# Prompt's spectral products on GpSimd, and an output projection that starts on half of its input

## The reference

```
def bidir_long_conv(u, filt):
    ...
    uf = jnp.fft.rfft(u.astype(jnp.float32), n=2 * L, axis=1)
    kf = jnp.fft.rfft(k2, n=2 * L, axis=0)
    return jnp.fft.irfft(uf * kf[None], n=2 * L, axis=1)[:, :L]

def hyena(...):
    u = h @ in_w + in_b
    up = jnp.pad(u, ((0, 0), (1, 1), (0, 0)))
    u = up[:, :-2] * conv_w[0] + up[:, 1:-1] * conv_w[1] + up[:, 2:] * conv_w[2] + conv_b
    x0, x1, v = jnp.split(u, 3, axis=-1)
    zz = v * x1
    y = bidir_long_conv(zz, filt).astype(h.dtype) + zz * dskip
    return (x0 * y) @ out_w
```

## Time and profile before

| | us |
|---|---|
| median of 3 runs (890.23 to 892.2) | 890.26 |
| the profiled execution | 887.65 |
| its span in the trace | 885.8 |
| TensorE busy | 833.5 (94%) |
| VectorE busy | 230.7 (26%) |
| ScalarE busy | 164.6 (19%) |
| GpSimd busy | 38.1 (4%) |

### The profile page before, as it was taken

One profiled execution on the slowest core, in us unless ns is written; L12 is line 12 of the kernel. 1 busy time (PEld: TensorE's weight loads), 2 busy tenths in 40 slices (PEclk: granted clock), 3 DMA queues, 4 the chain that ended last, 5 costly groups with the idle time before them and its releaser, 6 DMA issues.

```text
span 885.8 us, 13072 instructions
## 1 busy us (share of the span) xinstructions
PE 833.5 (94%) x5672; PEld 526.5 (59%) x5672; DVE 230.7 (26%) x462; ACT 164.6 (19%) x313; POOL 38.1 (4%) x67
## 2 busy tenths in 40 slices
PE   4899999899899999999996999999899999999997
PEld 3776777787654455535544888778654554355534
DVE  1245523504611011100103344491420111011003
ACT  3146113521510000000002211400311000000001
POOL 5000000030300000000000000000120000000000
PEclk9999999999999999999998999999999999999999
DMA  9979866734989999999999945537469999999991
GB/s 314 387 255 360 306 247 216 285 140 139 428 329 426 418 427 428 428 430 429 428 407 387 362 154 184 196 107 274 161 255 425 424 431 424 431 428 428 428 425 56
DMA packets 59969, 292.48 MB, mean 330 GB/s; under 512 B 2961, under 2 KB 5126, under 8 KB 47572
## 3 DMA queue, kind: packets, MB, share of 16 engines
q1 hardware_dynamic: 57908, 289.69, 81.8%
q0 software_dynamic: 768, 1.04, 0.5%
q10 hardware_dynamic: 1248, 1.08, 0.4%
HBM read 290.10 MB, written 1.70 MB: 329 GB/s over the span
## 4 chain that ended last, share of the span: by engine, by line
PE 73%; DMA 15%; DVE 6%; ACT 4%; issue 1%; SPq 0%; POOL 0%; DVEq 0%; POOLq 0%
PE ps L1821 21%; DMA ring<-in_moe_w_up 12%; PE ps L1844 9%; PE ps L1940 8%; PE ps L1405 5%; PE ps L1808 4%; PE ps L1862 4%; PE ps L1595 3%; PE ps L1683 3%; PE ps L1467 3%; PE ps L1450 2%; PE ps L1473 2%; DMA ring<-in_ab_in_w 2%; ACT arena L559 1%; DVE xT L1127 1%
## 5 line engine op out<-in xcount | busy, mean ns | idle before, releaser
L1821 PE MATMUL ps<-ring,arena 128*64 128x512 f32 x1024 | 224.2, 593 | 5.5 <-DMA ring<-in_moe_w_up 3.7
L1821 PEld LDWEIGHTS ps<-ring,arena 128*64 128x64 f32 x1024 | 77.4, 137 | 148.0 <-issue 146.0
L1844 PE MATMUL ps<-ring,arena 128*64 128x512 f32 x512 | 113.4, 595 | 1.1 <-ACT arena L782 1.1
L1940 PE MATMUL ps<-hT,ring 128*128 128x256 f32 x384 | 84.1, 380 | 0.3 <-ACT modT L621 0.3
L1940 PEld LDWEIGHTS ps<-hT,ring 128*128 128x128 f32 x384 | 72.6, 190 | 11.4 <-issue 1.2
L1844 PEld LDWEIGHTS ps<-ring,arena 128*64 128x64 f32 x512 | 36.2, 137 | 66.4 <-issue 63.1
L1239 DVE TENSOR_TENSOR arena<-ps,arena 128x256 f32<-128x256 f32 x32 | 18.1, 607 | 218.4 <-PE ps L1821 218.4
L1808 PE MATMUL ps<-arena 128*128 (+1 forms) x512 | 59.9, 275 | 2.1 <-ACT arena L767 2.1
L1808 PEld LDWEIGHTS ps<-arena 128*128 128x128 f32 x512 | 58.4, 192 | 2.2 <-DVE arena L1217 2.2
L1862 PE MATMUL ps<-arena 128*128 (+1 forms) x256 | 59.5, 386 | 0.0
L1405 PE MATMUL ps<-ring,csil 128*32 128x128 f32 x1536 | 51.9, 290 | 7.8 <-ACT modT L621 3.9
(11 more groups left out here) (294 smaller groups left out, 695.8 us busy)
## 6 DMA issues: line engine op xcount, KB each, us to landing
ring<-in_moe_w_gate SPq DMA_DIRECT2D x32, 2048.0 KB, 14.4
ring<-in_moe_w_up SPq DMA_DIRECT2D x32, 2048.0 KB, 17.3
ring<-in_moe_w_down SPq DMA_DIRECT2D x32, 2048.0 KB, 12.8
ring<-in_mod_w SPq DMA_DIRECT2D x24, 2048.0 KB, 11.9
ring<-in_ab_in_w SPq DMA_DIRECT2D x6, 2048.0 KB, 18.1
ring<-in_hy_in_w SPq DMA_DIRECT2D x6, 2048.0 KB, 17.3
ring<-in_ab_out_w SPq DMA_DIRECT2D x2, 2048.0 KB, 11.5
ring<-in_hy_out_w SPq DMA_DIRECT2D x2, 2048.0 KB, 8.4
```

The lines of the kernel that those rows point to most:

```text
L1821: ins = mm(bank(4 + w)[e * 64:e * 64 + 64, :], xg[:, k, e * 64:e * 64 + 64], unit(n + 2 * w + e)[:, k, :], start=(k == 0), stop=(k == KD - 1))
L1844: ins = mm(bank(6 + half)[e * 64:e * 64 + 64, :], hidT[:, f, e * 64:e * 64 + 64], down_unit(n + 4 + e)[:, f, half * 512:half * 512 + 512], ...
L1940: ins = mm(bank(4 + j % 4)[:, 0:256], unit(n)[:, k, (j % 4) * 128:(j % 4) * 128 + 128], hk(k), start=(k == KORDER[0]), stop=(k == KORDER[-1]))
```

## The change

VectorE no longer makes the prompt's product. GpSimd makes it, in six tensor_tensor instructions behind its work for the experts of layer 0; all their inputs and outputs lie in SBUF. VectorE makes only the sample's two halves, behind convolutions 21 and 22. TensorE's inverse transform of the prompt waits for GpSimd's semaphore. For the sample, VectorE's last two instructions are cut in two, four chunks of channels each, and the output projection's first group of matmuls waits for the first four before k = 0 and for the others before k = 4.

```
 # GpSimd, behind the gates of the experts, layer 0
+                if l == 0:
+                    pool.wait_ge(q["a_spec"], 2)
+                    (Ua, Ub), (ya, yb) = U0, YS[0]
+                    g.tensor_tensor(ya, Ua, H["KA"], ALU.mult)
+                    link(pool, "g_chain", g.tensor_tensor(yb, Ub, H["KB"], ALU.mult))
+                    g.tensor_tensor(ya, ya, yb, ALU.subtract)
+                    link(pool, "g_chain", g.tensor_tensor(Ub, Ub, H["KC"], ALU.mult))
+                    link(pool, "g_chain", g.tensor_tensor(yb, Ua, H["KB"], ALU.mult))
+                    g.tensor_tensor(yb, yb, Ub, ALU.add).then_inc(q["g_fb"], 1)
...
 # VectorE
-            def spectral(s, part):
-                if s:
-                    dve.wait_ge(q["t_spec"], 2)
-                    Ua, Ub = bank(0, 2), bank(2, 2)
-                else:
-                    dve.wait_ge(q["a_spec"], 2)
-                    Ua, Ub = U0
-                ya, yb = YS[s]
+            def spectral(part):
+                dve.wait_ge(q["t_spec"], 2)
+                Ua, Ub = bank(0, 2), bank(2, 2)
+                ya, yb = YS[1]
...
-                if 19 <= j <= 22:
-                    spectral((j - 19) // 2, (j - 19) % 2)
+                if j in (21, 22):
+                    spectral(j - 21)
...
-                L(v.tensor_tensor(z4, z4, bank(4 + 2 * s, 2).rearrange("p (k t) -> p k t", k=KD), ALU.add))
-                v.tensor_tensor(x04, x04, z4, ALU.mult).then_inc(q["d_r"], 1)
+                y4 = bank(4 + 2 * s, 2).rearrange("p (k t) -> p k t", k=KD)
+                for ks in [slice(0, 4), slice(4, 8)] if s else [slice(0, 8)]:
+                    L(v.tensor_tensor(z4[:, ks], z4[:, ks], y4[:, ks], ALU.add))
+                    v.tensor_tensor(x04[:, ks], x04[:, ks], z4[:, ks], ALU.mult).then_inc(q["d_r"], 1)
...
 # TensorE
             for s in range(NS):
-                pe.wait_ge(q["d_spec"], s + 1)
+                if s == 0:
+                    pe.wait_ge(q["g_fb"], 2)
+                else:
+                    pe.wait_ge(q["d_spec"], 1)
...
-            pe.wait_ge(q["d_r"], 2)
-            out_projection(OUT1_AT, [0, 1, 2, 3], lambda k: H["x0"][:, k * 256:k * 256 + 256], mod_step)
+            def mixed_ready(k8, k):
+                if k8 == 0 and k % 4 == 0:
+                    pe.wait_ge(q["d_r"], 2 + k // 4)
+            out_projection(OUT1_AT, [0, 1, 2, 3], lambda k: H["x0"][:, k * 256:k * 256 + 256], mod_step, mixed_ready)
```

More of the change, by code:

```diff
@@ L1308, in spectral @@
                     v.tensor_tensor(yb, yb, t1, ALU.add).then_inc(q["d_spec"], 1)
-                    dve.wait_ge(q["d_spec"], s + 1)
+                    dve.wait_ge(q["d_spec"], 1)
             for j in range(24):
@@ L1673, in _, with out_projection @@
             pe.wait_ge(q["a_cat"], 2)
-            def out_projection(at_unit, banks, src, between=lambda c: None):
+            def out_projection(at_unit, banks, src, between=lambda c: None, ready=lambda k8, k: None):
                 for half in range(2):
@@ L1682, in out_projection @@
                         for k in range(KD):
+                            ready(k8, k)
                             ins = mm(out, unit(n)[:, k, c * 128:c * 128 + 128], src(k), start=(k == 0), stop=(k == KD - 1))
```

## The result

The changed kernel takes 896.67 us (median of 14 runs) where the kernel before takes 891.88 on the same chips: ratio 1.0049, 95% interval 1.0036 to 1.0062, so 4.4 us slower (3.2 to 5.5). On the 890.26 of the forecast that is 894.6, the number predicted. A second comparison gave 1.0041 (1.0027 to 1.0055).

What follows compares the result with a forecast made beforehand. TensorE was taken as the bound, with 1.90 us of waits to win; turns between GpSimd and VectorE, less the split, gave +2.85 us, with the clock's fall +4.36, so 890.26 + 4.36 = 894.6 us, range 890.2 to 896.3.

Steps and rivals of the forecast that it cites:

- Only 1.9 us to win: TensorE stood still 1.21 us before the sample's inverse transform and 0.69 before the output projection; 1.90 us is all to win.
- VectorE and GpSimd take turns, for whole instructions: In convolutions 20 and 21 VectorE's six instructions alternate with GpSimd's six; VectorE 7.3 us late, TensorE idle 4.5 us.
- tensor_scalar takes turns too: First instruction of convolutions 20 and 21, one input at two elements a cycle, also waits for GpSimd; its turn 0.27 us.
- rival 2: tensor_scalar of convolutions 20 and 21 does not wait for GpSimd, two turns fewer: +0.4, 890.7 us; chance 0.15.
- GpSimd's instruction, 2.09 us: Each GpSimd tensor_tensor of 128 x 1024 for the prompt's product takes 2.09 us, 1.96 of it per turn.
- GpSimd in time for the first transform, 0.95 us to spare: GpSimd has the prompt's products at 583.98, 0.95 us before TensorE's prompt transform wants them; that wait stays hidden.
- The split, 0.5 us: Output projection starting on the sample's first four chunks gains 0.5 us, after four matmuls at 0.23 and a 0.2 us wait.
- +2.85: Delay in us of the output projection against 596.50, from turns and split, before any fall of the clock.
- The clock, 1.5 us: TensorE's clock falls to 1.2 GHz for about 3.4 us after the gap, losing 1.7 us; total from +2.85 to +4.36.
- The sum: Turns, split and clock together delay the output projection, and the end one for one, by 4.36 us: 894.6 us.

Runs made afterwards that it cites:

- left_out: Changed kernel with GpSimd's six instructions for the prompt's product deleted, TensorE's first transform reading Ua and Ub; ratio to the kernel before 0.9966, stage 23.88 us.
- split_taps: Kernel before, with the sample's last two instructions cut in two and the first tap of convolutions 20 to 23 on ScalarE; ratio 0.9970, stage 24.00 us.
- pool_halves: Changed kernel with GpSimd's six instructions cut into twelve of 512 columns; ratio to the kernel before 0.9992, stage 27.72 us.
- pairs: Separate kernel computing nothing of the reference: one GpSimd form beside one VectorE form per section; GpSimd's two-input 128 x 1024 product took 2.34 us alone.
- split_alone: Kernel before with only the sample's last two VectorE instructions cut in two and the projection starting on four chunks; ratio 0.9977, stage 25.35 us.
- pool_alone: Changed kernel without the split: GpSimd makes the prompt's product, the output projection waits for all of x0*y; ratio to the kernel before 1.0061, stage 32.79 us.
- clock_fill: Changed kernel with eleven matmuls of 512 columns, which nothing waits for, added between the two inverse transforms; ratio to the kernel before 1.0080, stage 33.40 us.
- clock_fill5: Changed kernel with five matmuls of 512 columns, which nothing waits for, added between the two inverse transforms; ratio to the kernel before 1.0036, stage 29.71 us.

## Why the prediction was right, point by point

- *Only 1.9 us to win*: right, and slightly low. left_out and split_taps take the stage down by 2.2 and 2.1 us.
- *VectorE and GpSimd take turns, for whole instructions*: right, by the ends in the trace, by pool_halves and by pairs. Six turns, strictly alternating, as listed.
- *tensor_scalar takes turns too* (rival 2 denied it): right. Its second one beside GpSimd took 2.32 us instead of 0.41 (579.73 to 582.05). The Trainium skill (GPSIMD Engine Reference, Key points) names contention with VectorE instructions in a 2-port perf mode or with two SBUF inputs. The trace agrees on the second (the taps, 2.46 us), and on the first if the doubled rate of the tensor_scalar is such a mode, which no row names.
- *GpSimd's instruction, 2.09 us*: mis-sized. It is 2.34. The slope from 2 and 128 elements was too small. The 2.36 us that the prediction estimated from a figure of the Trainium skill (GPSIMD Engine Reference, Performance versus the Vector engine), and did not use in the sum, was within 0.02 us. GpSimd holds a turn for 2.20 us instead of 1.96. VectorE's turns were put too high: 0.28 and 0.15 instead of 0.34 and 0.27. In sum a gap of 5.49 us instead of 4.5. The other terms of the turns came out: six of them, each asked for while the other engine was at work.
- *GpSimd in time for the first transform, 0.95 us to spare*: right that TensorE shows no wait worth the name, wrong that anything was to spare. GpSimd ended at 586.82, 14.68 us after the copy; TensorE had asked 14.54 us after it before the change. Its weight load stood idle for 0.22 us for GpSimd, and the transform ended 0.07 us later than before, counted from the copy (18.57 us against 18.50).
- *The split, 0.5 us*: right in sign, mis-sized. It is 0.76 alone (split_alone), and 1.05 in the changed kernel (pool_alone's stage less the changed one's; from single profiles), of which 0.28 is the transform, 6.09 us against 5.81. The prediction took a row of the profile for a matmul, "four matmuls at 0.23". A float32 matmul is two rows here: line 1683 makes 64 matmuls and has 128 rows. So the first four take 1.86 us and not 0.93, the wait of 0.2 us for the other chunks would not have arisen, and the prediction's own times then give 599.88 - 599.16 = 0.72 us for the split, close to what split_alone shows. The same misreading put clock_fill's matmuls at half their length. In the forecast it touches only the +2.85, which would have been +2.66; with the clock falling no such wait was in the sum.
- *The clock, 1.5 us*: right that it falls in such a gap. The transform lost 2.0 us rather than 1.7: it ran for 4.3 us at the lower clock (596.19 to 600.5) and not for the 3.4 taken over from the earlier trace rows.
- *The sum*: +4.36 was made for a stage that came out at +5.63, and met a timed +4.4. Of the 1.27 us between, 1.05 lie before the sample's transform (the turns) and 0.35 in it (the clock), with 0.13 back behind it. That the time agrees to 0.1 us is therefore luck; the microsecond between stage and time, seen in nearly every kernel of the table, was not predicted and stays open.

## What to carry to other kernels

Before elementwise work goes to GpSimd beside VectorE, list VectorE's instructions in that stretch, up to GpSimd's end and beyond it: in these runs each one with two inputs in SBUF, and the tensor_scalar with its doubled rate, waited for a whole GpSimd instruction when it came to one at work, while those with an input in PSUM did not. If it has to be done, cut GpSimd's instructions short; if VectorE is short by a microsecond and ScalarE is idle, as here, ScalarE is the better helper. Look first at how long the engine that sets the end really waits: VectorE led this chain for 20 us, and there were about 2 us to gain. And count what a row of the profile is before pricing a part of it: here two rows were one matmul.

## What the runs showed of the hardware

- GpSimd's one-input tensor_scalar makes VectorE wait as well: 1.09 and 1.14 us instead of 0.41 and 0.48 beside instructions of 1.05 us. The rows of the kernel before had shown turns only beside GpSimd's two-input instructions.
- A broadcast input makes GpSimd's tensor_tensor of 128 x 1024 quicker: 1.90 us against 2.34.
- VectorE's tensor_tensor with one input in PSUM keeps its time beside GpSimd (median 424 ns, alone 423 to 425), and the reduction shows no wait (419 to 421 ns).
- The granted clock fell in the gap of 5.49 us, and in pool_halves behind one of 1.94 us, when TensorE was at work again, but not behind the 1.19 us of clock_fill5. The length of a gap does not decide it alone: in the kernel before 3.46 us left it at full speed.
